# Another order of projections, scores and values in the mixing stage of a two-layer block

## The reference, cut to what matters

```python
z = xn @ w_in                                   # (256, 3212), cut into the parts below
# 6 stick-breaking heads of 64 channels
q, k = rms_norm(sb_q), rms_norm(sb_k)
zs = q @ k.T * 64**-0.5                         # per head, causal
log_keep = where(before, -softplus(zs), 0)
w = where(before, exp(log_sigmoid(zs) + reverse_cumsum(log_keep) - log_keep), 0)
y_sb = rms_norm(w @ sb_v)
# 6 mLSTM heads: scores times a decay matrix, causal, divided by a norm
mq, mk = silu(causal_conv(ml_qk)) split
num = ((mq @ mk.T) * exp(dmat - m)) @ ml_v ;  den = row sums of the same
y_ml = rms_norm(num / max(|den|, exp(-m))) * sigmoid(ml_o)
# spatial gating, 4 groups
u, v = gelu(sg_uv) split ; y_sg = rms_norm(u * (tril(sg_w) @ rms_norm(v) + sg_b))
x = x + concat(y_sb, y_ml, y_sg) @ w_out
```

## Time and profile before

| | |
|---|---|
| median of 3 runs | 2328.86 us (2324.53 to 2336.24) |
| profiled execution, its own time | 2322.81 us |
| its span, first to last instruction | 2320.8 us |
| mean granted clock of TensorE | 0.969 of full |
| PE busy | 2185.4 us, 94% of the span |
| DVE, ACT, POOL busy | 1210.0, 431.1, 464.1 us |
| the changed stretch, layer 1 | from 637.57 us, the first product of `z30`, to 696.92 us, the end of `so5` |
| the same in layer 2 | from 1518.07 us to 1576.80 us |

### The profile page before, as it was taken

How to read it: one execution, slowest core, us unless ns; L and a number is a source line. 1 busy time by engine, 2 the same in 40 slices (tenths; PEclk the granted TensorE clock), 3 DMA queues, 4 the chain that set the end, 5 groups by cost and what they waited for, 6 DMA issues and landing times. The chain is left out here.

```text
span 2320.8 us, 32591 instructions
## 1 busy us (share of the span) xinstructions
PE 2185.4 (94%) x13344; PEld 1951.6 (84%) x13344; DVE 1210.0 (52%) x2470; ACT 431.1 (19%) x1035; POOL 464.1 (20%) x410
## 2 busy tenths in 40 slices
PE   7998699998988999999999997998999999999998
PEld 4465488886667899999999997667899999999998
DVE  3255421112642796888644443542596877744443
ACT  3013310001241103443100000242112442200000
POOL 0000000000000013444533330000012444433331
PEclk9999899999988999999999998988999999999999
DMA  9135123443422488999999995322288999999996
GB/s 369 51 148 206 73 91 132 158 163 113 164 86 91 150 312 343 390 398 399 403 409 409 407 407 226 145 110 91 109 304 319 395 380 373 412 409 409 406 408 255
DMA packets 113525, 616.38 MB, mean 266 GB/s; under 512 B 10201, under 2 KB 10585, under 8 KB 95322
## 3 DMA queue, kind: packets, MB, share of 16 engines
q1 hardware_dynamic: 55578, 403.31, 44.3%
q0 software_dynamic: 57504, 208.82, 23.6%
q10 hardware_dynamic: 288, 2.10, 0.3%
HBM read 612.16 MB, written 2.03 MB: 265 GB/s over the span
## 5 line engine op out<-in xcount | busy, mean ns | idle before, releaser
L390 PE MATMUL psum<-HT,arena 128*128 128x160 f32 (+1 forms) x5984 | 994.0, 327 | 15.4 <-DVE HT L1644 7.1
L390 PEld LDWEIGHTS psum<-HT,arena 128*128 128x128 f32 x5984 | 924.7, 191 | 69.2 <-issue 18.3
L390 PE MATMUL psum<-arena 128*128 128x160 f32 (+6 forms) x5850 | 879.6, 312 | 37.2 <-DMA arena<-in_peer_v 13.9
L390 PEld LDWEIGHTS psum<-arena 128*128 128x128 f32 (+2 forms) x5850 | 814.2, 193 | 86.9 <-issue 32.3
L1962 DVE SCALAR_TENSOR_TENSOR arena<-arena,small 128x1024 f32<-128x1024 f32 x180 | 231.3, 1285 | 288.0 <-DMA arena<-in_peer_v,small 275.9
L2062 POOL DMA_INDIRECT arena<-in_peer_u,small x192 | 246.6, 1284 | 318.2 <-DVE small L1913 281.4
L2062 POOL DMA_INDIRECT arena<-in_peer_v,small x192 | 203.6, 1060 | 363.3 <-PE psum L390 206.9
L1913 DVE CUSTOM_DVE_ANT_0 arena<-arena 128x1024 f32<-128x1024 f32 x192 | 228.7, 1222 | 57.1 <-DMA arena<-in_peer_u,small 52.7
L2068 POOL DMA_DIRECT2D row_tokens<-arena x2 | 1.2, 623 | 1090.9 <-ACT arena L957 1090.9
L390 PE MATMUL psum<-arena,HT 128*128 128x384 f32 (+3 forms) x544 | 199.3, 526 | 7.0 <-DVE HT L1644 7.0
L957 ACT ACTIVATE arena<-psum 128x512 f32<-128x512 f32 (+6 forms) x130 | 64.9, 513 | 653.4 <-PE psum L425 333.3
(11 more groups left out here) (227 smaller groups left out, 996.6 us busy)
## 6 DMA issues: line engine op xcount, KB each, us to landing
arena<-in_peer_ut SPq DMA_DIRECT2D x64, 2048.0 KB
arena<-in_peer_v SPq DMA_DIRECT2D x64, 2048.0 KB
arena<-in_w_mod SPq DMA_DIRECT2D x12, 2048.0 KB
arena<-in_w_in SPq DMA_DIRECT2D x16, 1536.0 KB
arena<-in_w_up SPq DMA_DIRECT2D x11, 2048.0 KB
arena<-in_peer_wq SPq DMA_DIRECT2D x8, 2048.0 KB
arena<-in_w_out SPq DMA_DIRECT2D x6, 2048.0 KB
arena<-in_w_down SPq DMA_DIRECT2D x11, 1024.0 KB
```

Of the source, the lines that this page charges most:

```text
L390: return pe.matmul(o, a, b, start=start, stop=stop, skip_group_check=True)
```

## The change

Nothing is computed otherwise; the order of the work changes on three engines.

- PE: between `z30` and `z31` now come the transposes `sqk` and the mLSTM scores `ms`. Behind `z31` come the stick-breaking scores `sz`, the gating `sg` and the mLSTM values `mo`. Then `z20`, all six exponents `se`, `z21`, and all six values `so` in a row. The halves `z31` and `z20` now take their banks from 6 and 7, as `z21` did.
- ACT: `ML_W` comes ahead of the copy of `z30`; the copies of tile 3 and tile 2 follow PE's order; the copies of `mo` are gone; the squares of the mLSTM and gating outputs come ahead of the stick-breaking exponentials, and the copies of `so` all behind them.
- DVE: the multiplication of the mLSTM scores comes ahead of `sg_v` and `V1`, which has a semaphore of its own (`ml_v`). DVE copies `mo` out. The gating and mLSTM outputs come ahead of the stick-breaking log terms, and the sums of squares ahead of the loop over exponents.

```diff
@@ -702,7 +702,7 @@
                             between()
                             used_up.append(tile)
                         token_job(f"z{t}{b}", w, HT, b, 0, width, (s("l_normed"), 0) if (t, b) == (4, 0) else None,
-                                  (6, 7) if (t, b) == (2, 1) else range(8))
+                                  (6, 7) if (t, b) in ((3, 1), (2, 0), (2, 1)) else range(8))
...
@@ -738,8 +738,6 @@
                     e = EROW[0:MLH, h * P:(h + 1) * P]
                     mm(ps[:, 0:T], e, MROW[0:MLH, 1, :], True, True)
                     end(mm(ps[:, T:T + P], e, MROW[0:MLH, 1, P:T], True, True), f"mm{h}")
-                token_tile(3)
-
...
-                pe.wait_ge(s("ml_ready"), 2)
-                for h in range(MLH):
-                    ps = begin(f"ms{h}")
-                    causal_scores(ps, MQ, h, True)
-                    end(causal_scores_1(ps, MQ, h, True), f"ms{h}")
-
-                def all_sb_scores():
+                def scores_between():
                     pe.wait_ge(s("sbk_ready"), 1)
                     for g in range(3):
                         transposes(f"sqk{g}", [Z[:, b, (2 * g + j) * P:(2 * g + j + 1) * P]
                                                for j in range(2) for b in range(TB)])
-                    jobs.wait_read(pe, "sqk2")
+                    pe.wait_ge(s("ml_ready"), 2)
+                    for h in range(MLH):
+                        ps = begin(f"ms{h}")
+                        causal_scores(ps, MQ, h, True)
+                        end(causal_scores_1(ps, MQ, h, True), f"ms{h}")
+
+                def gating_and_ml():
+                    pe.wait_ge(s("ws_masked"), 1)
+                    pe.wait_ge(s("sg_v"), 1)
+                    for b in range(TB):
+                        ps = begin(f"sg{b}", (6, 7))
+                        for g in range(4):
+                            last = mm(ps[:, g * HD:(g + 1) * HD], WS[:, g, :],
+                                      Z[:, b, SG0 + 256 + g * HD:SG0 + 256 + (g + 1) * HD], True, True)
+                        end(last, f"sg{b}")
+                    pe.wait_ge(s("ml_v"), 1)
+                    for h in range(MLH):
+                        ml_values(h)
+
+                token_tile(3, between=scores_between)
+                jobs.wait_read(pe, "sqk2")
+                for h in range(SBH):
+                    sb_scores(h)
+                gating_and_ml()
+
+                def all_exponents():
                     for h in range(SBH):
-                        sb_scores(h)
-
-                token_tile(2, between=all_sb_scores)
-                for h in range(MLH):
-                    ml_values(h)
-
-                pe.wait_ge(s("ws_masked"), 1)
-                pe.wait_ge(s("sg_v"), 1)
-                for b in range(TB):
-                    ps = begin(f"sg{b}", (6, 7))
-                    for g in range(4):
-                        last = mm(ps[:, g * HD:(g + 1) * HD], WS[:, g, :],
-                                  Z[:, b, SG0 + 256 + g * HD:SG0 + 256 + (g + 1) * HD], True, True)
-                    end(last, f"sg{b}")
+                        sb_exponents(h)
+
+                token_tile(2, between=all_exponents)
                 jobs.wait_read(pe, "z21")
-                for h in range(SBH + 2):
-                    if h < SBH:
-                        sb_exponents(h)
-                    if h >= 2:
-                        sb_values(h - 2)
+                for h in range(SBH):
+                    sb_values(h)
...
@@ -1143,13 +1146,12 @@
                 act.activation(SQF[:, 1536:3072].rearrange("p (b c) -> p b c", b=TB), Z[:, :, 0:768],
                                ACT.Square).then_inc(s("sbk_squared"), 1)
                 root("sbk_rooted", small[:, 0:32], lambda: act.wait_ge(s("sbk_mean"), 1))
-                z_out(3)
                 act.wait_ge(s("ml_d"), 1)
                 act.activation(ML_W[:, :, :], ML_W[:, :, :], ACT.Exp, scale=-1.0).then_inc(s("ml_w"), 1)
                 jobs.wait_read(act, "mt")
                 act.activation(GA[:, 12:14, 0:MLH], GA[:, 10:12, 0:MLH], ACT.Exp,
                                scale=-1.0).then_inc(s("expm"), 1)
-                z_out(2, [0])
+                z_out(3, [0])
                 act.wait_ge(s("layer_params_in"), 32)
                 for g in range(3):
                     name = f"sqk{g}"
@@ -1159,6 +1161,7 @@
                         last = act.activation(QK2[:, 2 * g + j, :], bank(name)[:, j * T:(j + 1) * T], ACT.Copy,
                                               scale=CP2[:, c:c + 1])
                     last.then_inc(free(name), 1)
+                z_out(3, [1])
 
                 for h in range(SBH):
                     jobs.wait_full(act, f"sz{h}")
@@ -1171,22 +1174,18 @@
                 for h in range(0, SBH, 2):
                     act.activation(SB_W[:, h:h + 2, :], SB_W[:, h:h + 2, :], ACT.Ln, bias=1.0
                                    ).then_inc(s("sb_exp"), 1)
+                y2_squares = SQF[:, 0:2048].rearrange("p (b c) -> p b c", b=TB)
+                act.wait_ge(s("y2_done"), 1)
+                act.activation(y2_squares[:, :, 384:D], Y2[:, :, 384:D], ACT.Square
+                               ).then_inc(s("y2_squared"), 1)
+                z_out(2, [0])
+                for h in range(SBH):
+                    jobs.wait_read(act, f"se{h}")
+                    act.activation(SB_W[:, h, :], SB_W[:, h, :], ACT.Exp).then_inc(s("sb_wexp"), 1)
                 z_out(2, [1])
-                for h in range(MLH):
-                    copy_out(f"mo{h}", MB[:, :, h * 65:(h + 1) * 65],
-                             bank(f"mo{h}")[:, 0:130].rearrange("p (b d) -> p b d", b=TB))
-                y2_squares = SQF[:, 0:2048].rearrange("p (b c) -> p b c", b=TB)
-                for h in range(SBH + 2):
-                    if h < SBH:
-                        jobs.wait_read(act, f"se{h}")
-                        act.activation(SB_W[:, h, :], SB_W[:, h, :], ACT.Exp).then_inc(s("sb_wexp"), 1)
-                    if h == 3:
-                        act.wait_ge(s("y2_done"), 1)
-                        act.activation(y2_squares[:, :, 384:D], Y2[:, :, 384:D], ACT.Square
-                                       ).then_inc(s("y2_squared"), 1)
-                    if h >= 2:
-                        copy_out(f"so{h - 2}", Y2[:, :, (h - 2) * HD:(h - 1) * HD],
-                                 bank(f"so{h - 2}")[:, 0:P].rearrange("p (b d) -> p b d", b=TB))
+                for h in range(SBH):
+                    copy_out(f"so{h}", Y2[:, :, h * HD:(h + 1) * HD],
+                             bank(f"so{h}")[:, 0:P].rearrange("p (b d) -> p b d", b=TB))
                 for h in range(SBH):
                     jobs.wait_read(act, f"so{h}")
                 act.activation(y2_squares[:, :, 0:384], Y2[:, :, 0:384], ACT.Square).then_inc(s("y2_squared"), 1)
@@ -1730,18 +1729,6 @@
                 zqk = heads(Z[:, :, 0:768], 12)
                 dve.tensor_tensor(zqk, zqk, bc(st.unsqueeze(3), P, TB, 12, HD), ALU.mult
                                   ).then_inc(s("sbk_ready"), 1)
-                sgv = Z[:, :, SG0 + 256:SG0 + 512]
-                steps(dve.tensor_tensor(heads(sgv, 4), heads(sgv, 4), bc(
-                    small[:, 24:32].rearrange("p (b g) -> p b g", b=TB).unsqueeze(3), P, TB, 4, HD), ALU.mult))
-                dve.tensor_tensor(sgv, sgv, bc(CP2[:, C2["vng"]:C2["vng"] + 256].unsqueeze(1), P, TB, 256),
-                                  ALU.mult).then_inc(s("sg_v"), 1)
-
-                jobs.wait_read(dve, "z30")
-                jobs.wait_read(dve, "z31")
-                steps(dve.tensor_copy(heads(V1[:, :, :], MLH, 65)[:, :, :, 0:HD],
-                                      heads(Z[:, :, MLV0:MLV0 + 384], MLH)))
-                steps(dve.memset(heads(V1[:, :, :], MLH, 65)[:, :, :, HD:HD + 1], 1.0))
-
                 def diagonal(x, mask):
 
                     d = x.rearrange("p (c t) -> p c t", c=3)[:, 0:3:2, :]
@@ -1758,15 +1745,17 @@
                         diagonal(ML_W[:, h - 1, :], LE).then_inc(s("ml_p"), 1)
 
 
-                for h in range(SBH + 1):
-                    if h < SBH:
-                        dve.wait_ge(s("sb_exp"), h // 2 + 1)
-                        name, w = f"sz{h}", SB_W[:, h, :]
-                        dve.scalar_tensor_tensor(w, bank(name)[:, 0:384], 0.0, w, ALU.max, ALU.add
-                                                 ).then_inc(free(name), 1)
-                    if h >= 1:
-                        jobs.wait_read(dve, f"sz{h - 1}")
-                        diagonal(SB_W[:, h - 1, :], LT).then_inc(s("sb_spm"), 1)
+                sgv = Z[:, :, SG0 + 256:SG0 + 512]
+                steps(dve.tensor_tensor(heads(sgv, 4), heads(sgv, 4), bc(
+                    small[:, 24:32].rearrange("p (b g) -> p b g", b=TB).unsqueeze(3), P, TB, 4, HD), ALU.mult))
+                dve.tensor_tensor(sgv, sgv, bc(CP2[:, C2["vng"]:C2["vng"] + 256].unsqueeze(1), P, TB, 256),
```

(37 more changed lines are left out.)

## The result

The changed kernel takes 2298.11 us in the median of 4 runs (2292.72 to 2302.82), beside 2328.49 us for the kernel before on the same chip. The ratio is 0.9862, with a 95% interval of 0.9842 to 0.9882: 30.4 us less. Rival 1 gives 2305.4 us and is nearer than the forecast.

The account below looks back on a forecast made before the run. PE was taken to bound the mixing stretch. Per layer 45.9 + 0.1 + 0.4 + 2.5 + 0.9 = 49.8 us, so 18.4 us won over two layers: 2310.5 us from a median of 2328.9, range 2299 to 2320.

Parts of the forecast that it names:

- Rival 1: In `sg` and `mo`: the clock doesn't fall; layer 47.3 us, gain 23.5 us, whole 2305.4 us; chance 0.20.
- What bounds the stretch: Mixing stretch: PE sets its length by work, waits and clock; DVE and ACT matter only where PE waits for them.
- The waits: PE between `z30` and `so5`: four waits of 7.5 us go; 0.1, 0.4 and 0.9 us remain.
- Ahead of `z31`: PE waits for bank 6, held by `ms2` until DVE releases it: 0.1 us, the wait the change adds.
- Ahead of `so0`: PE waits until ACT has copied `z21`: 0.5 us and two hand-overs, 0.9 us.
- Bank waits in `mo`: Waits in `sg` and `mo`, 0.4 us together, range 0 to 1.5; DVE's copy bounded by 0.28 and 0.5 us.
- the narrow margin behind it: DVE's chain behind `mo5`, 14.2 us, lies under PE's 16.1 us of `z20`, `se`, `z21`: margin 1.9 us.
- The clock in `sg` and `mo`: 52 narrow passes in one block lose some clock: 2.5 us a layer, ends 0 and 5.3.
- The sum: A layer takes 49.8 us; layer 1 wins 9.5, layer 2 wins 8.9, together 18.4 us; whole 2310.5 us.
- Rivals 2 to 4: Rival 2: DVE becomes the bound; with 3 us more a layer, gain 12.4 us, whole 2316.5 us; chance 0.10.
- rival 3: Half clock wherever products are narrow, also in `so`: layer 55.1 us, gain 7.8 us, whole 2321 us; chance 0.06.
- rival 4: Clock stays down over `z20`, `se`, `z21` after the narrow block: layer 68.7 us, whole 2348 us; chance 0.04.

Follow-up runs that it names:

- The kernel with the gap: Changed kernel, with PE made to wait ahead of `mo0` until ACT's second exponential of the scores is done; 2311.47 us, ratio 0.9906 to the kernel before.
- the doubled one: Changed kernel, with each `mo` product issued twice into the same place and no gap; 2306.04 us, ratio 0.9885 to the kernel before.

## Why the prediction was right and where it failed

**What bounds the stretch: right.** PE sets it. The four waits of 7.5 us went, and what is left is PE's work, two waits of 1.1 us together and the half clock of `z30`.

**The waits: right in place and nearly in size.** Ahead of `z31` 0.56 us for 0.1, because DVE took up `ms0` later than I had it; the bank is indeed the wait that the change adds. Ahead of `so0` 0.58 for 0.9. Bank waits in `mo` are 0 to 0.15 us for 0.4: DVE's copy takes 0.29 us, at the lower of my two bounds. That `z20` covers the way to the first exponent is borne out (no wait), and so is the narrow margin behind it, in which DVE's delay showed at once. It is narrower than forecast: DVE's chain behind `mo5` took 15.0 us (669.77 to 684.78) where I had 14.2, beside 15.8 us of PE where I had 16.1; the wait in the version with the delayed DVE puts the margin at 1.1 us, not 1.9.

**The clock in `sg` and `mo`: the step that failed.** The prediction says: "I take 2.5 us, with 0 and 5.3 as ends." It is 0, in all six layers profiled. The row that I leaned on, 671.9 to 678.5 at 0.50, is a row behind a gap of 1.57 us, and I noted this and gave rival 1 only 0.20. The kernel with the gap gives 3.1 us of clock for it and the doubled one nothing, so the 2.5 us was a fair price for a gap that the change had removed. The Trainium skill ("TensorE: Matmul & The Clock Gate", section "Why this matters for your kernels") says that an engine kept busy without gaps holds its throughput, and on this block the trace agrees: 6.67 us at 1.00, with PE busy for 6.48, and 8.06 of 8.06 us with the products doubled. The same row of the page warns of long gaps only. Here a gap of 1.57 us ahead of the narrow products was enough to bring the clock down, and behind such a gap the kernel before kept PE busy for 6.60 of 6.60 us and still stood at 0.50; on both the measurement decides.

**Small prices: the other 1.4 us a layer.** I priced runs of narrow products by single groups of six, whose modelled last pass made them 0.13 us a pass; in a run of 36 it is 0.118. `se`, `sg`, `mo` and `so` together are 1.2 us shorter than forecast, the waits among them left out.

**The sum.** Of the 12.4 us between 2310.5 and 2298.1, the stretches account for 26.3 - 18.4 = 7.9: 5.0 for the clock, 2.9 for prices and waits. The other 4.5 are not in the stretches: outside them and the 9.5 us between `so5` and the output projection, the spans of before are 2183.6 and 2188.5 us, of after 2186.6, 2190.6 and 2183.6. They don't differ between the kernels by more than between executions of one. In part the 4.5 us are before's own swing. Its two profiled pairs of stretches are 118.1 and 120.9 us, mean 119.5, and after's three mean 92.2, so a typical execution loses 27.3 and not 26.3. The medians differ by 30.4, 28.5 and 33.0 us; the remaining 3 us are in no row of a profile. The granted clock of the other executions points to where they may be: the two profiled executions of before had 0.968 in the mean, all 48 of its executions whose clock was taken 0.966, and among these a thousandth of the clock goes with 1.6 us. By an estimate from these numbers, the profiles of before show it some 3 us too fast. In which stages, no run shows.

**Rivals 2 to 4.** DVE didn't become the bound, but was 1.1 us from it. Half clock wherever it is narrow (rival 3) fell with the doubled products; in `so` it was seen once in the kernel's six layers and cost 1.3 us. The clock didn't stay down in the wide work (rival 4): even where it had fallen in `mo`, it was back within `z20` (mean 0.82 there).

## What to carry to other kernels

Where the clock is at half beside a fully busy PE, look at what stands ahead of it before pricing it into the new order: a wait of 1.6 us cost another 3 us in the narrow products and the half tile behind it, and taking the wait away gave both back. Read the price of a product from a long run of the same kind, start to start, not from a group of six. And follow a won microsecond to the next wide stretch: in one version the half clock behind few-row products only moved to another tile, and in another the output projection opened at half clock and took back what the stretch had won.

## What the runs showed of the hardware that I had not expected

- Products 65 columns wide hold full clock for 8.06 us when nothing interrupts them. Behind a wait of 1.57 or 3.51 us they fell to half in all eight layers profiled, and so did products 64 wide behind one of 3.35 us, in both layers. At half PE is busy without a gap for 5.15 us and still at 0.50; it came back in the wide products that followed. A wait of 0.58 us ahead of `so` was enough in 2 of the 16 layers, over all versions, that have it, and so was one of 1.46 us ahead of `sz` with one of 0.36 us behind, in one layer of two. What decides there is open. Ahead of the scores `sz` of the kernel before, 256 wide and followed by a half tile, the same 1.57 us cost no clock (2.33 us for the 24 passes).
- The half clock behind products of 6 rows doesn't depend on the full length of that run: with 12 passes (2.2 us) in place of 24 (4.2 us) the half tile behind them took 7.1 us in three of four layers, 5.4 in the fourth. In five of the profiled layers with 24 passes the clock fell already within that run, which then took 5.0 to 5.3 us for 4.2.
- The output projection opened at 0.50 for 4.1 us behind 8 transposes and a wait of 1.08 us, in all four layers that have them. Behind 16 transposes, which themselves ran at 0.50, and a wait of 1.13 us it opened at 1.00 in layer 1 of the kernel after: there the granted clock rose in the wait, with PE idle (mean 0.73 from 698.60 to 699.74 us). In layer 2 of the kernel before it opened near half (0.55 over 4.2 us) behind the same. What decides is open.
- Copies of 128 x 130 values out of PSUM take 0.29 us on DVE and 0.28 us on ACT, so that the choice between them is one of queues alone.
